# Two of five token tiles: a dense coefficient matrix times the whole value table in place of gathered value rows, and a denser sample stage

## The reference, cut to what matters

```python
def peer(x, w_q, sub_keys, expert_u, expert_v):
    # x (N, 1024). Product-key retrieval per token and head;
    # output sum_h sum_k g v_e gelu(u_e.x)
```

## Time and profile before

| | us |
|---|---|
| median of three runs | 2445.83 (2444.44 to 2457.82) |
| span of the profiled execution | 2493.9 |
| its first gather, its last gather | 439.1, 2474.0 |
| TensorE, VectorE, ScalarE, GpSimd busy in it | 1810.2, 1433.9, 307.8, 1307.8 |
| moved by DMA | 791.9 MB, of it gathers 604.6 MB |

### The profile page before, as it was taken

The page is one execution under the profiler, slowest core; times in us unless marked ns, Lnnn a source line. Parts: engine busy times, 40 slices in busy tenths (PEclk is TensorE's granted clock), DMA queues, the critical chain, the costliest instruction groups (busy, mean ns, idle before and its releaser), DMA issues.

```text
span 2493.9 us, 23573 instructions
## 1 busy us (share of the span) xinstructions
PE 1810.2 (73%) x7244; PEld 768.0 (31%) x7247; DVE 1433.9 (57%) x3191; ACT 307.8 (12%) x732; POOL 1307.8 (52%) x1175
## 2 busy tenths in 40 slices
PE   9999988899699635566666766776777884555566
PEld 6767646644244201111112121221223250110011
DVE  2115876898845643999856569854444437434400
ACT  0214442111011101001101010110110010000000
POOL 1100000467655744555555557766777747677664
PEclk9998987999899867777778789998999997876678
DMA  5206322999989976999999999999999999999997
GB/s 182 71 3 195 102 85 68 355 328 410 361 306 368 346 281 238 394 367 400 386 401 380 401 371 362 371 356 368 378 384 409 409 370 374 364 359 380 355 377 287
DMA packets 259648, 791.92 MB, mean 318 GB/s; under 512 B 31522, under 2 KB 56163, under 8 KB 258947
## 3 DMA queue, kind: packets, MB, share of 16 engines
q0 software_dynamic: 166400, 604.58, 63.6%
q1 hardware_dynamic: 91268, 180.82, 20.6%
q10 hardware_dynamic: 1856, 5.03, 0.5%
HBM read 784.13 MB, written 5.59 MB: 317 GB/s over the span
## 4 chain that ended last, share of the span: by engine, by line
POOL 13%; DMA 10%; PE 8%; issue 7%; SPq 7%; another core or an unknown queue 6%; DVE 2%; ACT 1%; POOLq 0%
POOL arena L918 13%; DMA arena<-v_b 4%; PE ps L1369 3%; SPq L841 3%; DMA arena<-peer_v,arena 3%; SPq L768 2%; DMA arena<-peer_u,arena 2%; PE ps L1325 2%; DMA arena<-kv_a 2%; SPq L834 1%; PE ps L1202 1%; DVE arena L2081 1%; PE ps L1302 1%; ACT arena L1640 0%
## 5 line engine op out<-in xcount | busy, mean ns | idle before, releaser
L1369 PE MATMUL ps<-arena 128*32 128x512 f32 x2304 | 767.5, 717 | 346.6 <-DMA arena<-peer_v,arena 287.9
L2081 DVE CUSTOM_DVE_ANT_0 arena<-arena 128x1024 f32<-128x1024 f32 x576 | 694.7, 1225 | 531.5 <-DMA arena<-peer_u,arena 475.7
L918 POOL DMA_INDIRECT arena<-peer_v,arena x576 | 623.4, 1082 | 445.9 <-PE ps L1369 245.0
L918 POOL DMA_INDIRECT arena<-peer_u,arena x576 | 664.1, 1153 | 311.8 <-issue 162.2
L1369 PEld LDWEIGHTS ps<-arena 128*32 128x32 f32 x2304 | 153.4, 122 | 877.7 <-issue 662.1
L1164 PE MATMUL ps<-arena 128*128 128x448 f32 (+2 forms) x512 | 156.8, 467 | 13.1 <-DVE arena L1997 12.4
L1202 PE MATMUL ps<-arena 128*128 128x384 f32 (+2 forms) x704 | 146.5, 368 | 10.0 <-ACT arena L1576 8.1
L1325 PE MATMUL ps<-arena 128*64 128x512 f32 (+1 forms) x512 | 102.6, 538 | 68.1 <-DMA arena<-v_b 57.3
L900 POOL MEMSET arena<- 128x1024 f32 x1 | 1.0, 953 | 282.4 <-ACTq L723 282.4
L950 PE MATMUL ps<-arena 128*128 128x296 f32 (+1 forms) x512 | 132.1, 419 | 6.2 <-DMA arena<-xT 6.2
L1699 ACT ACTIVATE arena<-arena 128x8 f32<-128x8 f32 x72 | 15.3, 216 | 943.1 <-PE ps L1369 635.2
(11 more groups left out here) (211 smaller groups left out, 1694.1 us busy)
## 6 DMA issues: line engine op xcount, KB each, us to landing
arena<-k_b SPq DMA_DIRECT2D x128, 256.0 KB
arena<-v_b SPq DMA_DIRECT2D x128, 256.0 KB
arena<-w_mix SPq DMA_DIRECT2D x56, 512.0 KB
arena<-w_q SPq DMA_DIRECT2D x48, 512.0 KB
arena<-kv_a SPq DMA_DIRECT2D x128, 128.0 KB
arena<-w_out SPq DMA_DIRECT2D x24, 512.0 KB
arena<-peer_u,arena POOLq DMA_INDIRECT x576
arena<-peer_v,arena POOLq DMA_INDIRECT x576
```

The costliest lines, as they stand in the source:

```text
L918: pool.indirect_dma_start(out=rows[slot_of[n]], out_offset=None, in_=io["peer_v"] if v else io["peer_u"], in_offset=bass.IndirectOffsetOnA ...
L1369: last = pe.matmul(bank(6 + a, 512, 32 * lane, 32 * lane + 32), strips[:, GT * (G % 2) + k % GT, MID - r_:MID - r_ + 32], rows[slot_of[n]] ...
L2081: dve.tensor_tensor_reduce(out=row, in0=row, in1=h, scale=1.0, scalar=0.0, op0=ALU.mult, op1=ALU.add, accum_out=pre[:, k:k + 1]).then_inc( ...
```

## The change

Tiles 1 and 2 no longer gather value rows. In their place a matrix W[expert, token] is made on the chip and multiplied with the whole table `peer_v`, which SyncE reads once in its natural order, 128 loads of 128 consecutive rows (512 KB each, four buffers).

W comes in two halves of e0 (64 values each), each in 64 `build` items of four tokens. For a token, with its 128 picks on the partitions, VectorE makes the one-hot matrix of e1 (128 picks x 128) and that of e0 times the coefficient (128 picks x 64); TensorE multiplies them (contraction over the picks), and ScalarE copies four 128x64 results from PSUM into `w_dense`. Then 64 `dense` items: table block e (128 rows) as the moving operand, W[.., e] of tile 1 and of tile 2 as weights, 2 x 2 matmuls of 128x512, accumulated in PSUM banks 0 to 3 over all 128 blocks of the table.

The gathers are 896 now, and tile 2's and 3's u rows come with no v rows between. The sample stage keeps its pieces and their order, with all gaps times 0.43, the merge of tile 4 with gaps times 0.8; the top-k rounds are spread from one gather behind `admit` to eight behind `s_out` of q = 3. Row slots are ten throughout. The packing of tile 4 moves from SyncE's queue to ScalarE's. Names and numbers for both kernels:

| at gather number | before | changed |
|---|---|---|
| index products 0, 1, 2, 3 (`ix`) | 199, 236, 248, 264 | 198, 214, 219, 226 |
| top-k rounds, first and last | 278, 527 | 232, 337 |
| `s_out` of q = 3, q = 7 | 512, 744 | 333, 432 |
| merge of tile 4 | 764 to 840 | 441 to 501 |
| route of tile 3; of tile 4 | 522 to 597; 850 to 925 | 402 to 477; 530 to 605 |
| builds, first half; second | | 517 to 564; 694 to 742 |
| dense items, first 64; second 64 | | 565 to 692; 742 to 869 |
| last gather | 1151 | 895 |

Its core (line numbers aside, in the file's order):

```diff
-        later = vs[1] + vs[2] + vs[3]
+        DENSE, BY_ROW = (1, 2), (0, 3, 4)
         ALONE = 72
-        gathers = us[0] + vs[0][:ALONE] + weave(us[1], vs[0][ALONE:]) + weave(us[2], later[:120]) + weave(us[3], later[120:244]) + later[244:320]
-        gathers += weave(us[4], later[320:370]) + later[370:] + vs[4]
+        gathers = us[0] + vs[0][:ALONE] + weave(us[1], vs[0][ALONE:]) + us[2] + us[3]
+        gathers += weave(us[4], vs[3][:64]) + vs[3][64:] + vs[4]
...
+        SAMPLE_PACE, MERGE_PACE = 0.43, 0.8
...
         for item, gap in sample_items():
             put(at, *item)
-            q_at_[item[:2]] = at
-            at += gap
-        s_end = at
-        top_from, top_to = q_at_[("admit",)] + 2, q_at_[("s_out", 3)] + 24
+            q_at_[item[:2]] = int(at)
+            at += SAMPLE_PACE * gap
+        s_end = int(at)
+        top_from, top_to = q_at_[("admit",)] + 1, q_at_[("s_out", 3)] + 8
...
-        SWITCH = -(-(s_end + 24) // NR0) * NR0
...
+        BUILDS = 2 * 128 // GB
+        dense_items = [(("split",), 1.0)]
+        for h in range(2):
+            dense_items += [(("build", h, g), 1.3) for g in range(BUILDS)]
+            dense_items += [(("dense", h, e), 3.5) for e in range(HALF)]
+        d_from, d_to = max(m4_end + 2, turned_at[2] + 2), NG - 24
+        spent, whole = 0.0, sum(c for _, c in dense_items)
+        for item, cost in dense_items:
+            put(d_from + (d_to - d_from) * spent / whole, *item)
+            spent += cost
...
-            s_ = n % NR0 if n < SWITCH else (n - SWITCH) % NR
+            s_ = n % NR
...
+            def tables_of_values():
                 sp.wait_ge(sc_ready, 20)
+                for n in range(2 * HALF):
+                    if n >= NTB:
+                        sp.wait_ge(dense_used, n - NTB + 1)
+                    sp.dma_start(table[n % NTB], io["peer_v"][128 * n:128 * n + 128, :]).then_inc(table_loaded[n % NTB], 16)
...
+            def build(h, g):
...
+                pe.wait_ge(hot_ready, n + 1)
+                if n >= 2:
+                    pe.wait_ge(w_copied, n - 1)
...
+                for t in range(GB):
+                    last = pe.matmul(ps[:, c0 + HALF * t:c0 + HALF * (t + 1)], hot_j[n % NHOT][:, t, :],
+                                     hot_i[n % NHOT][:, t, :], start=True, stop=True)
+                last.then_inc(w_built, 1)
+
+            def dense(h, e):
...
+                if e == 0:
+                    pe.wait_ge(w_copied, BUILDS * (h + 1))
+                pe.wait_ge(table_loaded[n % NTB], 16 * (n // NTB + 1))
+                for t in range(2):
+                    for a in range(2):
+                        last = pe.matmul(bank(2 * t + a), w_dense[t][:, e, :], table[n % NTB][:, a * 512:(a + 1) * 512],
+                                         start=(n == 0), stop=(n == 2 * HALF - 1))
+                last.then_inc(dense_used, 1)
...
+                act.activation(w_dense[g // (BUILDS // 2)][:, :, t0:t0 + GB].rearrange("p e t -> p t e"),
+                               ps[:, c0:c0 + 256].rearrange("p (t e) -> p t e", t=GB), ACT.Copy).then_inc(w_copied, 1)
...
+                n, t, t0 = BUILDS * h + g, g // (BUILDS // 2), GB * (g % (BUILDS // 2))
+                if n >= NHOT:
+                    dve.wait_ge(w_built, n - NHOT + 1)
+                o_j, o_i = hot_j[n % NHOT], hot_i[n % NHOT]
+                dve.tensor_tensor(o_j, const("iota")[:, None, :].to_broadcast([128, GB, 128]),
+                                  col_no[t][:, t0:t0 + GB, None].to_broadcast([128, GB, 128]), ALU.is_equal)
+                step(dve.tensor_tensor(o_i, const("iota")[:, None, HALF * h:HALF * (h + 1)].to_broadcast([128, GB, HALF]),
+                                       row_no[t][:, t0:t0 + GB, None].to_broadcast([128, GB, HALF]), ALU.is_equal))
+                dve.tensor_tensor(o_i, o_i, coefD[t][:, t0:t0 + GB, None].to_broadcast([128, GB, HALF]), ALU.mult
+                                  ).then_inc(hot_ready, 1)
```

178 lines of the change are left out of this document (126 added, 52 removed).

## The result

The changed kernel takes **2635.8 us** (median of 4 runs, 2631.4 to 2645.5), the kernel before in the same group of runs 2451.8 (4 runs, 2444.4 to 2492.3). The ratio is 1.075 [1.069, 1.080]: slower by 184 us, where 64 had been forecast, and outside the forecast range (2395 to 2610). The sign was right and the size was not. The profiled execution has a span of 2643.7 us, so the sum of the stretches missed by 84 us (2560 was forecast); the other 42 us of the miss lie in how that sum was turned into a median.

A forecast was written before the change was run, and what follows sets the result against it. Bytes were taken to bound the kernel from 979 us on, bar one dip. Stretches summed to 2560 us against the profiled 2493.9, 66 us slower; carried to the 2446 median this gave 2510 us, range 2395 to 2610.

The forecast's parts named there:

- 178 us of bytes saved, given back as idle transfers: Whole kernel: net 67.1 MB less transfer saves 178 us, lost again under builds, last dense part, tight places and dip.
- 187: Gathers 512 to 565, the first 64 builds: VectorE sets the stretch at 187 us, against 79 us of bytes.
- 120 us: Gathers 694 to 743, the other builds: VectorE sets the stretch at 120 us, against 68 us of bytes.
- I take 300: Gathers 743 to 872, last dense items and value rows: TensorE 298 us, bytes 265, taken as 300 us.
- 108 + 52: Idle transfers under the two build stretches: 108 us in the first, 52 in the second.
- 230 to 341 [...] Two loads so near each other, plus softmax hand-offs: I take 345: Gathers 230 to 341, top-k rounds and FoX pairs: VectorE 312 us, bytes 330, taken as 345 us.
- 341 to 440: [...] 184: Gathers 341 to 440: 70 MB of bytes take 184 us, VectorE 155, so 184 us.
- The index products: Gathers 192 to 230: TensorE past the indexer keys at 945 us, 34 us sooner but 55 us poorer; loss 21 us.
- I carry the difference over: 2446 + 66: Final step: the 66 us slowdown against the profiled 2493.9 us is added to the 2446 us median, rounded to 2510.
- The bytes decide all the same: Rival: builds and dense products lie under transfers, 2280 us as a median; chance 0.2 together with a mixed case about 2400.
- Nothing to measure: Rival for the whole change: losses of 150 to 190 us against 178 saved, 2434 to 2458 us; chance 0.1.
- The dense products run at the low clock: Rival: TensorE's dense items, throttled by waits, lose 40 to 167 us, 2550 to 2680, put at 2600; chance 0.18.

The follow-up runs named there:

- press alone: Kernel before with only the sample stage's order changed (gaps times 0.43, tile 4 merge times 0.8, top-k rounds in a shorter stretch), all gathers kept: 2643.3 us, ratio 1.065.
- the pace 0.7: Kernel before with only the sample stage tightened as in press alone, but gaps times 0.7 in place of 0.43: 2479.4 us, ratio 1.031.

## Why the prediction came out as it did

**Right: the dense part.** "178 us of bytes saved, given back as idle transfers" is what the rows of the first chip show, with 66 MB fewer and nothing gained. The stretches of the builds, "187" and "120 us", came at 166 and 124, with VectorE 90% and 86% busy and the share at 0.60 and 0.70; the last one, "I take 300", at 308 with TensorE busy 307.4. Leaving VectorE's builds out gave 92 us. All seven stretches behind gather 440 together were off by 18 us, in part because misses cancel: the first builds came 21 us short and the stretch behind them 16 long, since TensorE finished the builds 33 us after gather 565 had gone out. What the forecast gave back under the builds, "108 + 52", is 80 and 46 by the same working (stretch less bytes at 0.38 MB a us). The sign "over 95% busy for some 180 us with the DMA share near 0.45" held for 150 us, from 1750 to 1900, with VectorE busy 49 of every 50 us and shares of 0.53, 0.45 and 0.46.

**Wrong: "230 to 341 [...] Two loads so near each other, plus softmax hand-offs: I take 345" and "341 to 440: [...] 184".** Between these gathers it took 388 and 232 us; counted as the forecast counted, from TensorE past the keys, 362 and 232. The heavier miss is the second, 48 us, where the sum had the bytes alone at full share and nothing for TensorE's waits for DSA pages, which came at 65.3 us. The first step took the larger of two loads (bytes 330, VectorE 312) and 15 us on top. One of the two loads was irrelevant: with 31 of 32 rounds gone the stretch took 385 us. The other, the bytes, was taken at full share here too. By the windows it is 0.89 x 388.1 = 345 us of transfers and 43 of idle engines in the first, 0.85 x 231.6 = 197 and 35 in the second. The waits point to what made the idle time, a coupling: TensorE works in its order, waits for pages (up to 12 us in FoX, 18 in DSA) and for the softmax chain, and with it wait the value sums and so the gathers, so that the queues of rows run dry. Shown is that the press makes the loss, that the rounds do not, that pages carry most of what could be taken back and the softmax scaling a little. That the order in front of the sums is what binds is argued from the waits: no run moved the sums or gave the page loads more room. The test that the text set itself ("takes far from 345 us, since there every engine waits for every other and my sum has only the two largest") named the weak place, but neither the sum nor a rival gave it a price. From the trace of before a price was at hand: it showed 0.82 of the share and 54.7 us of GpSimd's waits at the index products, where pieces stood densest, and the change put a whole stage at such a density. At 0.82 of 381 GB/s (377 / 0.99) the 125.3 and 70 MB take 401 and 224 us, and the stage ends at 945 + 625 = 1570 us, where 1474 was forecast and 1540 measured: too long by 30 instead of too short by 66. That is worked out afterwards, the 0.82 belongs to another wait (for indexer keys), and no run was made to test it as a rule.

**The index products** were forecast as a loss of 21 us, and the hole itself came as forecast (946.5 us with 236 gathers out). What their place costs the whole kernel is open: at their old gaps 26 us come back in the changed kernel, not clear of noise and with denser gaps behind them, and in press alone the ratio falls to 1.034, some 75 to 90 us if press alone stands at 1.065 to 1.071 on that chip too.

**Wrong: "I carry the difference over: 2446 + 66".** The profiled execution of before had a span of 2493.9 us, 48 above its median, and the sum was moved down by that. The changed kernel does not follow: profiled 2645.5, median 2635.8. A likely reason shows in the last 256 gathers of the old order, which are gathers alone. Kernel before on the first chip, and the pace 0.7 on that of the fourth group:

```profile
2098.80:2466.20 367.40, 204.53 (x773) 44.81 (x765) 117.16 (x250) 11.94 (x35) 255.91 (x256) 0.75 0.98 367
```

```profile
2131.80:2458.50 326.70, 191.16 (x761) 42.52 (x753) 116.41 (x249) 12.05 (x35) 246.03 (x256) 0.76 1.03 408
```

These are 367 GB/s and 408 GB/s with the same work. The other traces fall in line: 366 and 376 us for the two of press alone on the first chip, 324 to 325 for the three of the old order on the chip of the second group. In the trace of before it is 367.2, as on the first chip. A kernel that is bound by transfers gains some 40 us in this part alone; one that is bound by engines gains little. The difference should have been carried over only for stretches where bytes decide, and those are few in the changed kernel. That step makes 42 of the 126 us by which the median was missed, and the stage makes 64. That the runs of before were spread in this way is inferred, since no trace of a quick one exists.

**The rivals.** "The bytes decide all the same" is false, the share fell to 0.60 and 0.70 under the builds. "Nothing to measure" is true of the dense part taken alone on the first chip (7 us), and false of the change. (Two of its numbers were slips: losses of 150 us against 178 give 2418 us and not 2434, and the losses listed in one line add up to 241 and not 230.) "The dense products run at the low clock" is false at its place: with the first dense items the clock goes to 1.00, the third of these windows, and it is 0.98 over gathers 743 to 872:

```profile
1650.00:1700.00 50.00, 46.95 (x217) 46.05 (x217) 33.37 (x61) 6.22 (x18) 36.14 (x25) 0.50 0.91 334
1850.00:1900.00 50.00, 36.39 (x139) 31.15 (x140) 48.93 (x122) 10.43 (x18) 14.50 (x14) 0.51 0.46 137
1900.00:1950.00 50.00, 50.00 (x118) 22.02 (x118) 49.06 (x137) 1.79 (x3) 37.17 (x27) 1.00 0.95 369
```

But my reason against it ("low clock would make it busy all the time, and then the rows show the clock back at 1.00") does not hold in general. From 1650 to 1700 us TensorE is busy 47 of 50 us and the granted clock stays at 0.50, the 1.2 GHz level. It returned when the 512-column dense items came. The Trainium skill's "TensorE: Matmul & The Clock Gate", under "What's actually happening", says that the throttled state is the default and that activity releases the throttle. The trace agrees in part: the clock came back with work in the third row, and did not in the first, with 47 busy of 50 us. Nor is it the builds as such that keep it down: with VectorE's part left out, the second builds, which follow dense items, ran at 1.00 (the row 2109 to 2199 above). The cost is small: VectorE sets the stretch of the builds, and TensorE's 64-column work at half the clock only shows once the builds are left out (121 us at 0.50, TensorE busy 109).

**Open.** Why pages come late in the pressed stage was not separated: SyncE's loads go through a ring of four slots that TensorE frees, and they also share the engines with gathers. A run with a deeper ring would tell, and was not made. Nor are the 50 us lost behind gather 440 in the pressed kernel taken apart, nor the price of the ten slots, nor the dense part on a chip with faster gathers. Rounds and pages were never cut together.

## What to carry to other kernels

Where stages share one in-order engine with the work that frees transfer slots, the larger of two loads is a floor and not an estimate. Look for the transfers' share that the densest stage of the trace at hand reaches (0.82 here) and give the range room down to it; the share of the stages around it (0.99) was too kind by 66 us, the 0.82 too harsh by 30. Bytes saved are worth their time only where nothing else is near: here 66 MB fewer gave nothing that could be measured. And a profiled execution's distance to the median should be carried over, if at all, only for stretches with the same bound.

## What the runs showed of the hardware that was not expected

- TensorE's clock stayed at 0.50 of full speed while it was 94% busy (46.95 of 50 us), and in 109 busy of 121 us with builds of 64 columns; it was 1.00 with the dense items of 512 columns behind them. Builds of 64 columns that came after dense items ran at 1.00, busy 90.0 of 90 us.
- Gathers of 128 rows of 4 KB moved 367 GB/s on one chip and 408 on another, a difference of 11% with the same kernel order; the kernel before ran at 2477 and 2404 us there. The last 256 gathers took 366 to 376 us in three traces on the first chip (sixteen slots) and 324 to 327 in four traces on the two others. Whether the chip itself makes the difference, or something beside the kernel on it, is not shown.
